# Down projection of two of three token parts by seven products, its weight sums made in the first part; five PSUM banks for most gate and up pairs

## The reference

```python
u = rmsnorm(x, g_mix) @ w_in              # 1024 -> 3080: mLSTM heads and a short convolution
x = x + concat(h_m, y_c) @ w_out
f = rmsnorm(x, g_ffn)
x = x + (silu(f @ w_gate) * (f @ w_up)) @ w_down     # D_FF = 2816
e = rmsnorm(pe @ w_ple, g_ple)
x = x + sigmoid(x @ w_pg) * e
```

## Time and profile before

| | us |
|---|---|
| median of three runs | 2576.34 (2573.18 to 2578.26) |
| the profiled execution | 2572.7 |
| its span, first to last instruction | 2570.7 |
| TensorE busy | 2449.9 (95%) |
| VectorE busy | 1489.6 (58%) |
| ScalarE busy | 909.2 (35%) |
| GpSimd busy | 1011.5 (39%) |

### The profile page before, as it was taken

One profiled execution on the slowest core, in us unless ns is written; L12 is line 12 of the kernel. 1 busy time (PEld: TensorE's weight loads), 2 busy tenths in 40 slices (PEclk: granted clock), 3 DMA queues, 4 the chain that ended last, 5 costly groups with the idle time before them and its releaser, 6 DMA issues.

```text
span 2570.7 us, 40956 instructions
## 1 busy us (share of the span) xinstructions
PE 2449.9 (95%) x15757; PEld 2390.7 (93%) x15757; DVE 1489.6 (58%) x2327; ACT 909.2 (35%) x1694; POOL 1011.5 (39%) x785
## 2 busy tenths in 40 slices
PE   7899889999999999999999999998999999999998
PEld 6888778999999989999999999998899999999997
DVE  7668888656555684476643333468457763333355
ACT  5344443343334553334312122355134422221133
POOL 5655755576666342122322122333222232322233
PEclk9999999999999999999999999999999999999999
DMA  7556645576666746575555644575657555564544
GB/s 230 212 181 232 219 156 186 205 254 224 214 213 225 231 154 212 178 260 166 182 164 197 204 141 164 181 231 181 191 185 253 178 197 159 191 219 165 171 140 149
DMA packets 285043, 501.00 MB, mean 195 GB/s; under 512 B 18427, under 2 KB 182612, under 8 KB 284342
## 3 DMA queue, kind: packets, MB, share of 16 engines
q1 hardware_dynamic: 212182, 273.59, 31.5%
q10 hardware_dynamic: 72672, 224.82, 26.4%
HBM read 374.70 MB, written 123.65 MB: 194 GB/s over the span
## 4 chain that ended last, share of the span: by engine, by line
PE 69%; DVE 8%; DMA 5%; issue 2%; POOL 2%; ACT 1%; DVEq 0%; SPq 0%; ACTq 0%; POOLq 0%
PE bank L617 22%; PE bank L619 21%; PE bank L618 21%; DMA weight_parts<-wring 2%; DMA wring<-weight_parts 2%; POOL wring L2714 2%; DVE qlo L1807 1%; DMA xs<-x_prompt 1%; PE bank L754 1%; PE bank L809 0%; DVE qraw L2539 0%; PE bank L743 0%; DVE wide L2515 0%; DVE wraw L1797 0%; PE bank L732 0%
## 5 line engine op out<-in xcount | busy, mean ns | idle before, releaser
L2714 POOL TENSOR_TENSOR wring<-wraw,wring 128x512 fp32r<-128x512 f32 x525 | 767.6, 1470 | 1212.6 <-ACT wring L1293 1211.9
L617 PE MATMUL bank<-qhi,wring 128*128 128x352 f32 (+1 forms) x3540 | 1155.1, 326 | 74.6 <-DVE u L1861 14.0
L619 PE MATMUL bank<-qhi,wring 128*128 128x352 f32 (+1 forms) x3540 | 1138.4, 322 | 0.0
L618 PE MATMUL bank<-qlo,wring 128*128 128x352 f32 (+1 forms) x3540 | 1137.0, 321 | 0.0
L617 PEld LDWEIGHTS bank<-qhi,wring 128*128 128x128 f32 x3540 | 672.0, 190 | 99.7 <-issue 82.6
L618 PEld LDWEIGHTS bank<-qlo,wring 128*128 128x128 f32 x3540 | 671.8, 190 | 0.0
L619 PEld LDWEIGHTS bank<-qhi,wring 128*128 128x128 f32 x3540 | 669.8, 189 | 0.0
L1293 ACT ACTIVATE wring<-wraw 128x512 fp32r<-128x512 f32 x531 | 331.4, 628 | 717.1 <-PE bank L619 547.6
L617 PE MATMUL bank<-hid,wring 128*128 128x352 f32 (+1 forms) x1056 | 338.5, 321 | 5.2 <-DVE hid L2449 4.2
L619 PE MATMUL bank<-hid,wring 128*128 128x352 f32 (+1 forms) x1056 | 337.8, 320 | 0.0
L618 PE MATMUL bank<-hid,wring 128*128 128x352 f32 (+1 forms) x1056 | 337.0, 319 | 0.0
(11 more groups left out here) (322 smaller groups left out, 2389.0 us busy)
## 6 DMA issues: line engine op xcount, KB each, us to landing
wring<-weight_parts ACTq DMA_DIRECT2D x418, 512.0 KB, 4.5
weight_parts<-wring SPq DMA_DIRECT2D x201, 512.0 KB, 3.9
wraw<-w_down SPq DMA_DIRECT2D x33, 1024.0 KB, 7.3
wraw<-w_in SPq DMA_DIRECT2D x14, 1024.0 KB, 7.1
wraw<-w_gate SPq DMA_DIRECT2D x11, 1024.0 KB, 6.0
wraw<-w_up SPq DMA_DIRECT2D x11, 1024.0 KB, 6.0
wraw<-w_in SPq DMA_DIRECT2D x44, 256.0 KB, 4.9
wraw<-w_gate SPq DMA_DIRECT2D x44, 256.0 KB, 3.9
```

The lines of the kernel that those rows point to most:

```text
L617: nc.tensor.matmul(o, hi, mh, start=begins, stop=False, skip_group_check=True)
L618: nc.tensor.matmul(o, hi, ml, start=False, stop=False, skip_group_check=True)
L619: return nc.tensor.matmul(o, lo, mh, start=False, stop=ends, skip_group_check=True)
L2714: nc.gpsimd.tensor_tensor(wlo[e % RING][:, :].rearrange(v, k=k), w.src, whi[e % RING][:, :].rearrange(v, k=k), ALU.subtract).then_inc(lo_d ...
```

## The change

1. In parts 1 and 2, down groups 1 to 4 are made by seven products (`down_by_sevens`): two halves a of 512 output columns, seven products each, a product for two output columns m with its own four banks (all eight in use); a product is 2 x 2 x 3 = 12 matmuls. Group 0 and group 5 stay plain, and part 0 stays plain throughout.
2. The operands are seven in place of four: the hidden parts and T1 to T4, made from `sl` in float32 on VectorE, with ScalarE's high copies and VectorE's low parts. They lie where `hid` was (`dhi`, `dlo_first`) and in the space of raw buffers 2 and 3 (`dlo_rest`, `draw`).
3. So parts 1 and 2 have two raw buffers instead of four: SP issues raw r in step r, not r + 2.
4. The sums S1 to S4 of w_down (4 groups x 2 halves x 4 = 32) are made in part 0 from the group's own raws and stored; with the pg sums there are twelve spare entries per group instead of four: four after the pieces of the first half, three in the second, three in the up pair behind it, two in the gate pair after that. In parts 1 and 2 they are loaded.
5. Gate and up pairs get five banks (6 and 7 added) and the order `FIRST_PRODUCTS`, but for up 1, gate 2 and up 2. ScalarE's wait for the hidden part of channel 0 moves from the fourth product to the second.
6. From raw 26 on, SP in part 0 issues the stores of raw r - 1 before the next raw, which is r + 1 instead of r + 2.

```diff
+DOWN_SEVEN = (1, 2, 3, 4)
+DOWN_SPARES = (0, 1, 2, 3), (1, 2, 3), (0, 3, 6), (2, 5)
+PG_SPARE_LOADS = {24: 0, 29: 1, 35: 2, 41: 3}
+DOWN_BANKS = ((6, 7, 3, 4), (5, 2, 0, 1))
...
+        b = r % 2 if q else r % RAW_RING          # add_raw
...
-        if st == "gate":
-            return (0, 1, 2, 6, 7) if i == 0 else (0, 1, 2)
-        if st == "up":
-            return (3, 4, 5)
+        if st in ("gate", "up"):
+            own = (0, 1, 2) if st == "gate" else (3, 4, 5)
+            return own if (st, i) in (("up", 1), ("gate", 2), ("up", 2)) else own + (6, 7)
...
+            def down_by_sevens(q, g):             # TensorE
+                begins = ("P1", "P6", "P5", "P7", "P4")
+                for a in range(2):
+                    for name in DOWN_PRODUCTS:
+                        e, op = n_entry[0], OPERAND_OF[name]
...
+                        entry_ready(e)
+                        if not a:
+                            pe.wait_ge(h_lo, down_operand_low(q.n, g, op))
+                        for m in range(2):
...
+                            take(bk)
+                            for k in range(2):
+                                last = three(bank[bk][:, 0:q.N], hi[:, k, m, :], lo[:, k, m, :], dhi[:, op, k, 0:q.N],
+                                             down_low(op)[:, k, 0:q.N], name in begins and k == 0, k == 1)
...
                 for r in range(RAWS):             # SP
-                    raw()
+                    now = q.n * RAWS + r
+                    if not q.n and r > 25:
+                        keep_parts((now - 1,))
+                    raws_to(now if q.n else r + 2 if r < 26 else r + 1)
...
                 def after(s):                     # ScalarE, gate_after
                     if s == 0 and p:
                         hidden_high(q, p - 1, 0)
-                    if s == 3 and p:
-                        act.wait_ge(h_lo, HIDDEN[(q.n, p - 1, 0, None)])
+                    if s in (1, 2) and p % 2 and seven_pair(q.n, p - 1):
+                        for name in (("T1", "T2"), ("T3", "T4"))[s - 1]:
+                            difference_high(q, p - 1, name)
+                    if p and s == (3 if p == 2 else 1):
+                        act.wait_ge(h_lo, HID_LOW[(q.n, p - 1, last_hidden(q.n, p - 1, 0))])
...
+            def hidden_parts(q, p, c):            # VectorE; an even pair
...
+                nc.vector.tensor_tensor(dlo_rest[:, 0:2, c, 0:q.N], u, dhi[:, 1:3, c, 0:q.N], sub).then_inc(h_lo, 1)
+                dve.wait_ge(h_lo, HID_LOW[(q.n, p - 1, (c, "T1"))])
+                nc.vector.tensor_tensor(t_2, u[:, 1], t_1, sub).then_inc(h_lo, 1)
+                nc.vector.tensor_tensor(t_3, u[:, 1], t_3, sub).then_inc(h_lo, 1)
+                dve.wait_ge(h_lo, HID_LOW[(q.n, p, (c, "T2"))])
+                nc.vector.tensor_tensor(t_4, u[:, 0], t_2, sub).then_inc(h_lo, 1)
...
+                    if s in (1, 2, 5, 6) and p % 2 and seven_pair(q.n, p - 1):      # VectorE, gate_after
+                        difference_low(q, p - 1, {1: "T1", 2: "T2", 5: "T3", 6: "T4"}[s])
...
+                            if name == "P2":      # VectorE, down_by_sevens
+                                nc.vector.tensor_tensor(x[0, 0], x[0, 0], b1, add).then_inc(f1, 1)
+                                dve.wait_ge(*drained[key + ("P7",)])
+                                nc.vector.tensor_tensor(x[1, 1], x[1, 1], w, add)
+                                made_["x10"] = released[kw_] = own(nc.vector.tensor_tensor(x[1, 0], x[1, 0], w, add))
```

More of the change, by code:

```diff
@@ L454, in build, with spares_of, add_down @@
     ALL4, ALL2 = slice(0, 4), slice(0, 2)
-    def add_down(g, n=None):
-        if g == 0:
-            add_plain(w_down_v[:, 0:2, :], 2, D, [(ALL2, slice(256 * n, 256 * n + 256)) for n in range(4)])
+    down_raws = {}
+    def spares_of(q, w, p):
+        g = p // 2 if w == "down" else (p - 1) // 2
+        if q or g not in DOWN_SEVEN:
+            return {}
+        of = [("pg", g - 1)] * 4 + [("down", g, 0)] * 4 + [("down", g, 1)] * 4
+        turn = {("down", 0): 0, ("down", 1): 1, ("up", 1): 2, ("gate", 0): 3}.get((w, p % 2))
+        if turn is None:
+            return {}
+        before = sum(len(js) for js in DOWN_SPARES[:turn])
+        return {j: of[before + k] for k, j in enumerate(DOWN_SPARES[turn])}
+    def add_down(q, g):
+        if g == 0:
+            add_plain(q, w_down_v[:, 0:2, :], 2, D, [(ALL2, slice(256 * n, 256 * n + 256)) for n in range(4)])
+            return
+        if down_seven(q, g):
+            for a in range(2):
+                r, buf = add_raw(q, [(slice(0, 2048), w_down_v[:, 4 * g - 2:4 * g + 2, 512 * a:512 * a + 512])])
+                for p in DOWN_PRODUCTS:
+                    name = WEIGHT_OF[p]
+                    if name in ("A11", "A12", "A22"):
+                        add_entry(r, by_quarters(buf)[name], 0, name == "A11")
+                        end[r] = n_prepared[0]
+                    else:
+                        n_loads[0] += 1
+                        entries.append(Entry(r, None, 0, False, None, None, kept_as[(("down", g, a), name)]))
+                        entries[-1].loads = n_loads[0]
             return
         for a in range(2):
-            add_plain(w_down_v[:, 4 * g - 2:4 * g + 2, 512 * a:512 * a + 512], 4, 512,
-                      [(ALL4, slice(P * j, P * j + P)) for j in range(4)], {1: n, 3: n + 1} if a and n is not None else None)
+            down_raws[("down", g, a)] = len(raws)
+            add_plain(q, w_down_v[:, 4 * g - 2:4 * g + 2, 512 * a:512 * a + 512], 4, 512,
+                      [(ALL4, slice(P * j, P * j + P)) for j in range(4)], spares_of(q, "down", 2 * g + a))
     for q in supers:
@@ L1076, in raw, with raws_to @@
                     return
[L1077 to L1078 removed]
+                if raw_before[r] is not None:
+                    sp.wait_ge(lo_done, raw_end[raw_before[r]])
                 for where, src in raws[r]:
[L1080 to L1081 removed]
+                    sp.dma_start(wraw[raw_buffer[r]][:, where].rearrange("p (k n) -> p k n", k=src.shape[1]), src)\
+                        .then_inc(landed[raw_buffer[r]], 16)
+            def raws_to(r):
+                while n_raw[0] <= r:
+                    raw()
             def keep_parts(which, names=None):
@@ L1288, in one_ahead @@
                 if w.first:
[L1289 removed]
+                    act.wait_ge(landed[raw_buffer[w.raw]], raw_landed[w.raw])
                 if w.total:
@@ L2863, in _ @@
                     if down_before(p) is not None:
-                        for k in range(8 if down_before(p) else 4):
+                        for k in range(14 if down_seven(q.n, down_before(p)) else 8 if down_before(p) else 4):
                             ahead()
```

250 lines of the change are left out of this document (184 added, 66 removed).

## The result

The kernel after takes 2595.07 us (median; 2593.02 to 2605.13), the kernel before in the same series 2578.26 us: the ratio is 1.0075, with a 95% interval of 1.0058 to 1.0092. The forecast was 2562 us, with 2552 to 2571 as its own range and eight chances in ten for 2545 to 2584, so the change is slower where a gain was forecast, and the time lies outside both. The profiled execution of the kernel after took 2593.02 us.

The account below looks back on a forecast made before the run. TensorE, busy 95% of the span, was taken as the limit in parts 1 and 2, with a tight five-slot ring in part 0. Terms -30.0 + 6 + 3 + 7 = -14 us gave 2562 us, range 2552 to 2571.

Parts of the forecast that it names:

- The matmuls taken out, -30: Parts 1 and 2, four down groups each: 24 fewer matmuls per group take 30.0 us off TensorE at unchanged pace.
- VectorE's additions in a group, nothing: Down groups of parts 1 and 2: 36 additions, 18.8 us, fit beside 26.7 us of products, costing nothing.
- The operand chain, +6: Gates in parts 1 and 2: the seventh product's load, queued behind ScalarE's wait, lands 0.75 us late at eight places.
- the loads, +3: Parts 1 and 2: 64 more loads with a raw beside them add 3 us of waits, range 0 to 6.
- Part 0, +7 from -8 to +27: Part 0 with 32 more sums: +8 even gate pairs, -3 five banks, +2 VectorE crowding, together 7 us longer.
- The five banks ... I take -3: Part 0, pairs given five banks: TensorE's 7.9 us shared-bank waits lose their cause; -3 us, range 0 to -7.9.
- Crowding of VectorE by eight sums a cycle, +2: Part 0: eight more VectorE sums per cycle cost 2 us, including any remaining lateness of raws.
- In the odd up pair ten entries go through five slots: ... 11.2 us, under its 13.4: Part 0, odd up pair: with stores landing in 3.4 us the ring needs 11.2 us, under the pair's 13.4.
- Two sums now sit in that pair, so that the slot of the first product is wanted by the fifth, 1.9 us earlier ... I take 2.7 us more in each of the three cycles: Part 0, even gate pair behind two raws: earlier slot demand and less lead cost 2.7 us in three cycles, +8 us.
- the ring as the bound of part 0: Rival: up and gate entries make the five-slot ring bound part 0; slower, 2603 us at L = 8; chance 0.12.
- the signs listed as wrong: TensorE idle in groups on VectorE; idle odd up pairs; part 0 median landing over 6 us; part 0 over 15 us longer or unchanged.

Follow-up runs that it names:

- e1: Kernel after without part 0's sums of the down pieces; parts 1 and 2 load kept gate sums instead: 2549.73 us, 0.9892 of the kernel before.
- e6: Kernel before with only the five banks, the new product order for gate and up, and the earlier wait for hidden parts: 2571.06 us, ratio 0.9978.
- e2: Kernel after with gate and up pairs back on three banks and the old product order: 2615.29 us, 1.0148 of the kernel before.
- e8: Kernel after without VectorE's 32 additions for the down sums in part 0; unsummed pieces still prepared, stored and loaded: 2591.87 us, 1.0067 of the kernel before.
- e10: Kernel after, down sums in part 0 added and taking ring slots, but not prepared by ScalarE or POOL nor stored: 2576.64 us, 0.9994 of the kernel before.
- e3: Kernel after with ScalarE in part 0 copying P1 out before preparing the piece four ahead: 2592.97 us, 1.0059 of the kernel before.
- e13: Kernel after with P1's copy first, w_pg one piece later, and sums moved to (1, 3) in up and (5, 6) in gate: 2588.95 us, 1.0045 of the kernel before.

## Why the prediction was wrong

**The matmuls taken out, -30.** Right. Group 1 of part 1 runs from 1360.0 to 1386.8 us, 26.8 where 26.7 was worked out.

**VectorE's additions in a group, nothing.** Right: TensorE waited for nothing from 1358.5 to 1390 us.

**The operand chain, +6, and the loads, +3.** Right in place and, together, in size. In part 1 TensorE stands before the seventh product of gates 3, 5, 7 and 9; the first of them:

```profile
1358.02 0.43 PE L706 MATMUL bank<-qhi,wring 128*128 128x352 f32 x1 [1.70 <-DMA wring<-weight_parts]
```

With the others (1.5, 1.0 and 0.2) it is 4.5 us in part 1, in part 2 2.8 us at the same product: 7.2 where 6 were due. Other waits for loads are 3.3 us, all in part 2. The 0.5 and 3.6 us of the earlier trace rows that the prediction calls TensorE's waits are those of the weight load (PEld), which overlaps the matmuls. TensorE itself waited for loads 1.4 us before, all in part 2 (first line, 2042 to 2498 us); the other lines are the kernel after, parts 1 and 2:

```profile
PE bank L617 <- DMA wring<-weight_parts: 1.4, 3, 0.8
...
PE bank L706 <- DMA wring<-weight_parts: 4.5, 4, 1.7
...
PE bank L706 <- DMA wring<-weight_parts: 6.1, 8, 1.6
```

So loads cost 9.2 us more, where 9 were allowed. Parts 1 and 2 still gave 16.0 us together and not 21: matmuls take 0.5% and 0.3% longer (454.61 / 2836 against 467.04 / 2928 us, 437.75 / 2832 against 451.98 / 2932), 3.4 us, and the first plain group waits 1.5 us longer for VectorE; neither was in the sum. -30 + 9.2 + 3.4 + 1.5 = -15.9 accounts for them. Why the matmuls take longer no run shows; slow starts after waits (0.43 us above, where 0.32 is usual) are a part of it.

**Part 0, +7 from -8 to +27: this step failed; it was +34.** The sums were put at +10 (+8 and +2) and cost 43.7 us by e1; what comes with the five banks gave 9.6 back, not 3. Its terms:

- "The five banks ... I take -3": -5.8 by e6, and 7.4 us of part 0 in the kernel after by e2. Too small, on the safe side.
- "Crowding of VectorE by eight sums a cycle, +2": 1.5 by e8.
- "In the odd up pair ten entries go through five slots: ... 11.2 us, under its 13.4": wrong. TensorE waits 2.1 to 2.4 us in every one. The landing of 3.4 us from the earlier trace rows did not hold: the stores there now go out behind a raw of 1 MB and take 5.0 us (lines below). With 5.0 the same sum is 10 / 5 x 7.2 = 14.4 us, over the 13.4.
- "Two sums now sit in that pair, so that the slot of the first product is wanted by the fifth, 1.9 us earlier ... I take 2.7 us more in each of the three cycles": the place and the reason are right, and e10 shows that the slot alone makes ScalarE stand there. The size was not: 4.8 us in each of three cycles and 2.9 in the fourth, against 1.06 in the earlier trace rows. I let the lost lead count as time only. But ScalarE has the copy of the first product queued behind that wait, and the new order of products wants that bank at the third product instead of the fifth. I named what is queued behind ScalarE's wait in parts 1 and 2 and did not do it in part 0. That is where the loss shows; with the copy ahead of the wait (e3) part 0 is as long, so the price is the slot's and not the copy's.
- Nothing in the sum stood for the clock. After six of the eight longer waits TensorE ran its next 10 to 15 matmuls at the lower level: 10.4 us.

DMA issues around the first odd up pair of the four cycles, from 506 to 522 us (count, size, median us to landing), beside the earlier trace rows; SP issues the raw at 511.3 us and the stores from 512.6 on:

```profile
weight_parts<-wring SPq DMA_DIRECT2D x6, 512.0 KB, 5.0
wraw<-w_gate SPq DMA_DIRECT2D x1, 1024.0 KB, 7.3
```

**The rival that came nearest** was the slower one, the ring as the bound of part 0, with 2603 us and a chance of 0.12. Its place was right; its condition was not met: it asked for a median landing over 6.2 us, and the median was 3.6. The ring bound by the few stores behind the raws and by the slot itself, not by the mean. Of the signs listed as wrong, two came (idle time in the odd up pairs, part 0 longer by over 15 us); the landing and idle time inside the groups did not.

What stays open: that the sum's slot, and not one of the edits beside it, brings the stop at the even gate rests on e1 and e10 at one place; in e13 the copy goes first too, so that run does not show it by itself. Nor is it settled which wait makes up the rest in e13. Each cure of one stall met others of up to 5 us, on POOL, VectorE or the copy, and no run separates these.

## What to carry to other kernels

Work put in slack still needs the shared slots: before adding entries to a ring, count for each step whose slot it takes, when that one's store lands, and what the in-order engine that waits has queued behind the wait. Fill-in work that nobody needs soon is best kept out of the ring altogether, even if it is then finished later (here 44 us became 4 in part 0, at some 8 us more in the later parts). A short wait of TensorE is to be priced with the slow matmuls that can follow it.

## What the hardware showed that I had not expected

The granted clock fell after waits of a few microseconds in the middle of dense work, though not after all of them. After 2.21 us in the odd up pair of the first cycle of the kernel after (the wait ends at 522.26) it fell, after 2.37 us in that of the fourth (it ends at 810.00) it did not:

```profile
512.00:522.00 10.00, 8.05 (x51) 7.76 (x49) 5.56 (x6) 3.80 (x7) 7.78 (x7) 1.00 0.97 325
522.00:527.00 5.00, 4.74 (x20) 4.77 (x21) 1.12 (x2) 1.71 (x4) 2.82 (x3) 0.66 0.67 271
527.00:532.00 5.00, 5.00 (x33) 5.00 (x32) 3.17 (x7) 2.05 (x4) 4.52 (x4) 1.00 0.45 171
...
805.00:810.00 5.00, 2.63 (x18) 2.37 (x16) 3.35 (x2) 1.76 (x4) 4.39 (x4) 1.00 1.03 417
810.00:815.00 5.00, 5.00 (x31) 5.00 (x32) 1.93 (x4) 2.28 (x5) 3.90 (x4) 1.00 0.61 247
```

The wait of 2.21 us costs another 1.6 us (12 matmuls at 0.134 us too much), those of 2.9 to 4.9 us cost 1.5 to 2.2 us each; after the 0.8 us in a down group the clock stayed at 1.00. Of the four waits of 2.1 to 2.4 us two were followed by the lower level, in e8 all four (2.2 to 2.6 us); what decides it no run here shows. The Trainium skill (TensorE: Matmul & The Clock Gate, section "HAM oscillation — how this bites in real kernels") describes a kernel whose TensorE falls to half clock at every wait for a transfer and starts each burst cold; the trace agrees for its four waits of 2.9 to 4.9 us, here for ScalarE's copy, and for two of the four shorter ones.
